# Retention's first projection tiles inside the prompt's attention, and the sample rows scaled before the constants arrive

## The reference

```python
h = rms_norm(x, g_mix[l])
proj = jnp.einsum('bld,de->ble', h, w_in[l])
rq, rk, rv, rg, mq, mk, mv, gate_r, gate_a = split_proj(proj)
rq = retnet_rotate(rq.reshape(B, L, R_HEADS, R_DK), pos)
rk = retnet_rotate(rk.reshape(B, L, R_HEADS, R_DK), pos) * (R_DK ** -0.5)
ro, r_state = ret_mix(l, rq, rk, rv)              # chunkwise retention
mq = rope(mq.reshape(B, L, M_HEADS, M_DH), pos)
mk = rope(mk.reshape(B, L, M_HEADS, M_DH), pos)
mo = attn_mix(l, mq, mk, mv)                      # block-sparse softmax attention
merged = sigmoid(gate_r) * (ro @ w_br_ret[l]) + sigmoid(gate_a) * (mo @ w_br_att[l])
x = x + merged @ w_out[l]
x = x + (silu(gate) * up) @ w_down[l]             # gate, up = rms_norm(x, g_ffn[l]) @ w_gu[l]
```

## Time and profile before

| | us |
|---|---|
| median of three runs | 2099.04 |
| profiled execution, its own time | 2107.27 |
| its span, first to last instruction | 2105.7 |
| TensorE busy in the span (matmuls) | 2042.1 |
| VectorE busy | 972.5 |
| ScalarE busy | 685.5 |
| GpSimd busy | 127.5 |

### The profile page before, as it was taken

One profiled execution on the slowest core, in us unless ns is written; L12 is line 12 of the kernel. 1 busy time (PEld: TensorE's weight loads), 2 busy tenths in 40 slices (PEclk: granted clock), 3 DMA queues, 4 the chain that ended last, 5 costly groups with the idle time before them and its releaser, 6 DMA issues.

```text
span 2105.7 us, 45102 instructions
## 1 busy us (share of the span) xinstructions
PE 2042.1 (97%) x17393; PEld 1913.4 (91%) x17393; DVE 972.5 (46%) x1620; ACT 685.5 (33%) x1054; POOL 127.5 (6%) x211
## 2 busy tenths in 40 slices
PE   6989999999999999999999899999999999999999
PEld 5958878988999999999988688789899999999998
DVE  5573522456445544543354643133654544444433
ACT  4365423223223222222233654222322322222222
POOL 0001120011000000000000011200100000000000
PEclk9999999999999999999999999999999999999999
DMA  6316683245333233223344266813543323232222
GB/s 191 121 43 212 191 276 106 81 141 171 102 109 93 80 91 89 80 70 95 95 132 139 68 209 205 292 42 99 159 145 110 91 81 99 80 89 78 83 82 90
DMA packets 257967, 253.20 MB, mean 120 GB/s; under 512 B 12266, under 2 KB 223378, under 8 KB 257554
## 3 DMA queue, kind: packets, MB, share of 16 engines
q1 hardware_dynamic: 240050, 190.68, 29.7%
q0 software_dynamic: 17632, 60.31, 9.0%
q10 hardware_dynamic: 128, 0.15, 0.0%
HBM read 230.52 MB, written 20.58 MB: 119 GB/s over the span
## 4 chain that ended last, share of the span: by engine, by line
PE 90%; DVE 3%; issue 2%; ACT 2%; DMA 2%; SPq 1%; ACTq 0%; DVEq 0%; POOL 0%; POOLq 0%
PE PS L626 61%; PE PS L607 3%; PE PS L765 3%; PE PS L608 2%; PE PS L609 2%; PE PS L588 2%; PE PS L589 2%; PE PS L590 2%; PE PS L776 1%; PE PS L825 1%; PE PS L567 1%; PE PS L722 1%; DMA CL<-in_consts_layer 1%; PE PS L736 1%; PE PS L659 1%
## 5 line engine op out<-in xcount | busy, mean ns | idle before, releaser
L626 PE MATMUL PS<-XH,WH 128*128 128x272 f32 x2176 | 455.2, 290 | 5.0 <-DVE EA L1698 3.1
L626 PE MATMUL PS<-XH,WL 128*128 128x272 f32 x2176 | 451.1, 289 | 0.0
L626 PE MATMUL PS<-XL,WH 128*128 128x272 f32 x2176 | 449.4, 288 | 0.0
L1405 DVE TENSOR_TENSOR WL<-RAW,WH 128x2048 fp32r<-128x2048 f32 (+2 forms) x144 | 310.7, 2158 | 244.0 <-ACT WH L1045 243.2
L626 PEld LDWEIGHTS PS<-XH,WH 128*128 128x128 f32 x2176 | 342.2, 189 | 12.6 <-DVE EA L1698 8.2
L626 PEld LDWEIGHTS PS<-XL,WH 128*128 128x128 f32 x2176 | 342.1, 189 | 0.0
L626 PEld LDWEIGHTS PS<-XH,WL 128*128 128x128 f32 x2176 | 339.9, 189 | 0.0
L1045 ACT ACTIVATE WH<-RAW 128x2048 fp32r<-128x2048 f32 (+2 forms) x152 | 274.6, 1806 | 91.0 <-PE PS L626 88.0
L1647 DVE TENSOR_TENSOR EA<-PS,RSTDB 128x544 f32<-128x544 f32 x120 | 86.4, 722 | 227.0 <-PE PS L626 226.3
L1242 ACT ACTIVATE EB<-EA 128x544 f32<-128x544 f32 x92 | 60.5, 658 | 329.7 <-DVE EA L1647 276.0
L607 PE MATMUL PS<-WH,XH 128*128 128x256 f32 x512 | 152.3, 298 | 0.0
(11 more groups left out here) (266 smaller groups left out, 3071.6 us busy)
## 6 DMA issues: line engine op xcount, KB each, us to landing
RAW<-in_w_in SPq DMA_DIRECT2D x106, 512.0 KB, 4.5
RAW<-in_w_gu SPq DMA_DIRECT2D x88, 512.0 KB, 4.8
PG<-in_cache_k SPq DMA_DIRECT2D x64, 256.0 KB, 3.3
PG<-in_cache_k POOLq DMA_DIRECT2D x64, 256.0 KB, 3.3
RAW<-in_w_down SPq DMA_DIRECT2D x32, 384.0 KB, 3.3
PG<-in_cache_v SPq DMA_DIRECT2D x44, 256.0 KB, 4.7
PG<-in_cache_v POOLq DMA_DIRECT2D x44, 256.0 KB, 5.0
RAW<-in_w_down SPq DMA_DIRECT2D x32, 320.0 KB, 3.7
```

The costliest lines, as they stand in the source:

```text
L626: last = pe.matmul(PS[:, 2 * pair + h, 0:HALF], w[:, i, c0:c0 + P], x[:, k, h * HALF:(h + 1) * HALF], start=first and i == 0 and a == 0, s ...
L1405: dve.tensor_tensor(WL[:, slot, 0:n], RAW[:, slot, 0:n], WH[:, slot, 0:n].bitcast(F32), ALU.subtract).then_inc(lo_ready, 1)
```

## The change

1. **The head of a layer.** The copy of the sample rows to `XTD` is issued by ScalarE at the top of the layer, no more by SyncE. SyncE loads `CL` right behind the first two units, and saves the prompt's rows behind the third unit's load. VectorE scales `XN` before it waits for `CL`.
2. **The prompt's attention.** `spread` comes behind `scores(0)` and `scores(1)`, `take_rt` behind `row_max(0)` and `row_max(1)`. Then follows `rqk` tile 0, now a full tile, in PSUM bank 1; ScalarE reads it out in step 2, VectorE rotates it behind the attention. `rqk` tile 1, the sample tile of the first unit, runs in step 15 between `attend(14)` and `turn_probs(15)`.
3. **The two later stages.** All other `rqk` tiles run one place earlier. The last one no longer stands at the start of the value stage. The first value step holds `rv` tiles 0, 1 and 2, and each later tile moves up by one step, so that the last step holds none. Splits and four weight loads move with them.

```diff
-ORDER0 = tuple(range(TT - 2)) + (TT - 1, TT - 2)
+ORDERS = {"mqk": tuple(range(TT - 2)) + (TT - 1, TT - 2), "rqk": (0, TT - 1) + tuple(range(1, TT - 1))}
...
+    def row_bank(name, f):
+
+        return 1 if (name, f) == ("rqk", 0) else (6, 3)[f % 2]
...
-        u, i = divmod(g * N_PAGES + p, TT - 1)
-        return [u * TT, u * TT + 1] if i == 0 else [u * TT + 1 + i]
+        step, out = g * N_PAGES + p, []
+        for r in ((0, 1) if step == 0 else (step + 1,) if step + 1 < 4 * (TT - 1) else ()):
+            u, i = divmod(r, TT - 1)
+            out += [u * TT, u * TT + 1] if i == 0 else [u * TT + 1 + i]
+        return out
...
-        return q + 1 if q < N_PAGES else q + 3
+        return q + 2 if q < N_PAGES else q + 4
...
-            hold(sp, x_lo, lay * NX + KT)
-            sp.dma_start(XTD.ap()[:, :, SEQ:N], XN).then_inc(xs_kept, 16)
             hold(sp, tile_done, lay * NT + 1)
             sp.dma_start(CL[:], consts_layer).then_inc(cl_in, 16)
-            sp.dma_start(XTD.ap()[:, :, 0:SEQ], XT[:, :, 0:SEQ]).then_inc(xt_kept, 16)
             for j in range(2):
                 full(U0["mqk"] + 2 + j, j, w_in, KT, C_MQ + (2 + j) * UC)
+                if j == 0:
+                    hold(sp, x_lo, lay * NX + KT)
+                    sp.dma_start(XTD.ap()[:, :, 0:SEQ], XT[:, :, 0:SEQ]).then_inc(xt_kept, 16)
...
-                for at_r, name, j, col in ((2, "rqk", 2, C_RQ), (8, "rqk", 3, C_RQ), (12, "rv", 0, C_RV),
-                                           (16, "rv", 1, C_RV), (20, "rv", 2, C_RV), (24, "rv", 3, C_RV),
-                                           (28, "br_att", 0, C_GA)):
+                for at_r, name, j, col in ((2, "rqk", 2, C_RQ), (7, "rqk", 3, C_RQ), (12, "rv", 0, C_RV),
+                                           (15, "rv", 1, C_RV), (20, "rv", 2, C_RV), (23, "rv", 3, C_RV),
+                                           (27, "br_att", 0, C_GA)):
...
             transposes([rows_of(QK, j) for j in range(8)], 0, sample_kv)
-            spread(2 * lay + 1, (6, 7))
...
             scores(0)
             scores(1)
+            spread(2 * lay + 1, (6, 7))
+            pe.wait_ge(own_act, lay * 2 + 2)
+            token_part("rqk", 0, kk)
             for s in range(16):
                 if s + 2 < 16:
                     scores(s + 2)
                 if s:
                     attend(s - 1)
+                if s == 15:
+                    pe.wait_ge(s_exp, lay * 16 + 15)
+                    token_part("rqk", 1, kk)
                 turn_probs(s)
...
             turn_sample_probs(0)
-            token_part("rqk", 19, kk)
...
+            act.wait_ge(x_lo, lay * NX + KT)
+            act.dma_start(XTD.ap()[:, :, SEQ:N], XN).then_inc(xs_kept, 16)
             for u in range(4):
...
+                if s == 2:
+                    to_rotate(0)
...
+                if f == 2 * TT - 1:
+                    split_at("rqk", 3)
...
             sample_probs_turned(0)
-            to_rotate(19)
             exp_group(1)
...
                 ahead("mqk", u // 2, u % 2)
                 if u == 0:
+                    dve.wait_ge(xs_kept, lay * 16 + 16)
+                    dve.tensor_tensor(XN, XN, GT[:, bass.ds(lay * KT, KT)].unsqueeze(2).to_broadcast([P, KT, NS]),
+                                      ALU.mult).then_inc(xn_ready, 1)
                     dve.wait_ge(cl_in, lay * 16 + 16)
...
             row_max(0)
             row_max(1)
+            take_rt(2 * lay + 1, (6, 7))
```

More of the change, by code:

```diff
@@ L29, with row_tile @@
 ORDER = (TT - 1,) + tuple(range(TT - 1))
-ORDER0 = tuple(range(TT - 2)) + (TT - 1, TT - 2)
+ORDERS = {"mqk": tuple(range(TT - 2)) + (TT - 1, TT - 2), "rqk": (0, TT - 1) + tuple(range(1, TT - 1))}
 KG = P // NS
-def row_tile(f, first=False):
-    return f // TT, (ORDER0 if first and f < TT else ORDER)[f % TT]
+def row_tile(name, f):
+    return f // TT, (ORDERS.get(name, ORDER) if f < TT else ORDER)[f % TT]
 UC = 256
@@ L370, in unit @@
                 if isinstance(u, int) and 2 <= u < U0["br_att"] + 2:
-                    hold(sp, tile_done, lay * NT + T0["mqk"] + (u - 2) * TT + (ORDER0.index(TT - 1) if u == 2 else 0) + 1)
+                    hold(sp, tile_done, lay * NT + T0["mqk"] + (u - 2) * TT + {2: ORDERS["mqk"].index(TT - 1), U0["rqk"] + 2: ORDERS["rqk"].index(TT - 1)}.get(u, 0) + 1)
                 for dst, src in parts:
@@ L571, in first_tile @@
             def first_tile(f):
-                u, t = row_tile(f, True)
+                u, t = row_tile("mqk", f)
                 n = ROWS[t]
@@ L593, in token_part @@
             def token_part(name, f, ks):
-                u, t = row_tile(f)
+                u, t = row_tile(name, f)
                 n = ROWS[t]
@@ L598, in token_part @@
                 wl = WL[:, u % 2, :].rearrange("p (k c) -> p k c", c=UC)
-                out = PS[0:n, (3, 6)[f % 2], 0:UC]
+                out = PS[0:n, row_bank(name, f), 0:UC]
                 if ks[0] == 0:
@@ L603, in token_part @@
                 if t == TT - 1:
-                    last = sample_part(u, (3, 6)[f % 2], (0, 1) if len(ks) == KT else (ks[0] // 4,))
+                    last = sample_part(u, row_bank(name, f), (0, 1) if len(ks) == KT else (ks[0] // 4,))
                 for k in ks if t < TT - 1 else ():
@@ L731, in attend @@
                     pe.wait_ge(mo_lo, lay * 4 + hp - 1)
+                elif t == 0 and hp == 0:
+                    pe.wait_ge(own_act, lay * 2 + 1)
                 elif t == 0:
-                    pe.wait_ge(own_act, lay * 2 + hp + 1)
+                    pe.wait_ge(tile_free, lay * NT + T0["rqk"] + 3)
                 for kt in range(t + 1):
@@ L786, in key_scores @@
                     last.then_inc(sc_done, 1)
-            token_part("rqk", 0, kk)
             pe.wait_ge(mo_lo, lay * 4 + 4)
@@ L793, in _ @@
                 if q == N_PAGES:
-                    token_part("rqk", N_PAGES + 1, kk)
                     token_part("rqk", N_PAGES + 2, kk)
+                    token_part("rqk", N_PAGES + 3, kk)
                 if q + 1 < NG * N_PAGES:
@@ L1061, in to_rotate @@
             def to_rotate(f):
-                u, t = row_tile(f)
+                u, t = row_tile("rqk", f)
                 act.wait_ge(tile_done, lay * NT + T0["rqk"] + f + 1)
                 act.wait_ge(rot_free, lay * 40 + 20 + f + 1)
-                act.activation(XS[:, f % 2, :], PS[:, (3, 6)[f % 2], 0:UC], ACT.Copy,
+                act.activation(XS[:, f % 2, :], PS[:, row_bank("rqk", f), 0:UC], ACT.Copy,
                                scale=(RT if u < 2 else RTK)[:, t:t + 1]).then_inc(tile_free, 1)
@@ L1079, in _ @@
                 for f in range(u * TT, (u + 1) * TT):
-                    t = row_tile(f, True)[1]
+                    t = row_tile("mqk", f)[1]
                     done(T0["mqk"] + f)
@@ L1088, in _ @@
                 for f in range(j * TT, (j + 1) * TT):
-                    t = row_tile(f)[1]
+                    t = row_tile("mv", f)[1]
                     value_tile("mv", f, MV[:, t, :] if t < TT - 1 else MVP, first_bank(4 * TT + f))
@@ L1170, in _ @@
             split_at("rqk", 1)
-            to_rotate(0)
+            to_rotate(1)
             keys_turned(0, range(GRP))
@@ L1174, in _ @@
                 if q == N_PAGES:
-                    to_rotate(N_PAGES + 1)
-                    split_at("rqk", 3)
                     to_rotate(N_PAGES + 2)
+                    to_rotate(N_PAGES + 3)
                 if q + 1 < NG * N_PAGES:
@@ L1481, in _ @@
                 last.then_inc(tr_dve, 1)
-            take_rt(2 * lay + 1, (6, 7))
             def row_max(s):
@@ L1582, in sample_probs_turned @@
                 dve.tensor_copy(PTS[g][0:NS, 8, :], PS[0:NS, 2, 0:P]).then_inc(pts_dve, 1)
+            rotated(0)
             split_at("rqk", 1)
-            rotated(0)
+            rotated(1)
             for q in range(NG * N_PAGES):
@@ L1588, in _ @@
                     select(0)
-                    rotated(N_PAGES + 1)
-                    split_at("rqk", 3)
                     rotated(N_PAGES + 2)
+                    rotated(N_PAGES + 3)
                     inverse_sum(0)
@@ L1600, in _ @@
             sample_probs_turned(0)
-            rotated(19)
             inverse_sum(1)
```

12 lines of the change are left out of this document (4 added, 8 removed).

## The result

| | median us | spread, runs | profiled execution |
|---|---|---|---|
| before | 2099.29 | 2096.23 to 2104.84, 20 | 2107.27, span 2105.7 |
| after | 2104.34 | 2101.02 to 2107.79, 20 | 2102.82, span 2101.2 |

The changed kernel takes 1.0023 of the time before (95% interval 1.0015 to 1.003): 3.1 to 6.3 us slower, where 2.2 us faster (2096.8 against 2099.04) was forecast. The time lies above the forecast's range. Note the last column: in the two profiled executions the changed kernel is the faster one by 4.5 us. The profiled execution of before was slower than every one of its 20 timed runs, that of after is among its faster ones. Much of what follows comes from that.

The account below looks back on a forecast made before the run. TensorE, busy 97% of the span, was taken as the bound, so only its stops and lower clock could change. Terms -8.0 - 4.9 + 2.1 + 8.4 = -2.4 us gave 2096.8 us against 2099.04, range 2090.5 to 2102.5.

Parts of the forecast that it names:

- The head (-8.0): Head of both layers: stops of 2.18 and 2.83 us and 1.5 us of lower clock each go, 8.0 us gained.
- The carry-over: Whole kernel: the -2.4 us worked out on the profiled 2107.27 us applies unchanged to the median of 2099.04.
- The attention (-4.9 + 2.1): Prompt's attention, both layers: 4.9 us gained at its start by filling idle time, 2.1 lost at its end.
- The shift at the start: Start of the prompt's attention: a full tile of 3.05 us delays the chain by only 0.6, gaining 2.45 per layer.
- The tail's 1.05: End of the prompt's attention: the sample tile, moved ahead of `turn_probs(15)`, loses 1.05 us per layer.
- The key stage (0): Key stage: the moved split of unit 3 costs nothing; up to 1 us a layer if its cover fails.
- The value stage (+8.4): Start of the value stage: a new 2.7 us TensorE stop plus 1.5 of lower clock per layer, 8.4 us lost.
- attention takes nothing for free: Rival: attention carries every inserted piece in full, losing 6.8 us at its end; +4.7, 2103.7 us, slower; chance 14%.

Follow-up runs that it names:

- e1: Kernel before with only the head's part of the change (sample rows copied by ScalarE and scaled before the constants, early `CL` load): 2097.74 us, ratio 0.9982.
- e0: Kernel before, unchanged, profiled once more: 2101.19 us, ratio 1.0006; profiled execution 2100.78 us.
- e2: Changed kernel with the head's part undone, leaving the attention's tiles and the shifted later stages: 2107.03 us, ratio 1.0024.
- e5: Kernel before with only `spread` and `take_rt` moved behind scores 0 and 1 and their `row_max`, no tile moved: 2097.58 us, ratio 0.999.
- e4: Changed kernel with the first `rv` read-out ahead of `exp_group(1)` and the `CL` load held until x's low halves are written: 2094.72 us, ratio 0.9966.
- e6: Changed kernel with the first `rv` read-out ahead of `exp_group(1)` and the sample tile back behind `attend(15)`: 2094.45 us, ratio 0.9972.
- e7: Kernel before with the head's part, late `CL` load, and `spread` and `take_rt` behind scores 0 and 1; no `rqk` tile moved: 2094.87 us, ratio 0.9969.
- e8: Changed kernel with first `rv` read-out ahead of `exp_group(1)`, late `CL` load and sample tile back behind `attend(15)`: 2092.37 us, ratio 0.996.
- e9: Changed kernel, unaltered, timed again on the chip of another group of runs: 2103.81 us, ratio 1.0015.
- e3: Changed kernel with ScalarE reading out the first `rv` tile ahead of `exp_group(1)` instead of behind it: 2096.01 us, ratio 0.9976.

## Why the prediction was wrong

**What the profiles add up to.** Means over the layers of all profiled executions that share the piece in question (in brackets how many layers; for the changed head those with the early load):

| stretch, per layer | old form | changed form | old - changed | forecast |
|---|---|---|---|---|
| head, layer 0 (first matmul to second sample tile) | 17.8 (5) | 16.1 (5) | 1.7 | 3.7 |
| head, layer 1 | 17.8 (5) | 16.3 (5) | 1.5 | 4.3 |
| attention to first keys, and the full tile that left the value stage | 56.9 + 3.05 (8) | 58.2 (10) | 1.7 | 1.4 |
| value stage, `turn_sample_probs(0)` to the last product with `MVS`, the full tile that left it added | 76.5 (8) | 76.8 + 3.05 (6) | -3.4 | -4.2 |

**The head (-8.0) is the step that failed.** e1 measured -3.8 by its ratio and -2.5 by its medians, and the table's two rows give -3.2. In layer 0 the step read a stop of 2.18 us and 1.5 us of lower clock from one execution. The stop depends on when `CL` lands; in five executions with the old head it was 2.0 to 2.2 us in three, where `CL` landed 8.4 to 8.5 us after its issue, 0.47 in e0 and absent in e2, where it landed after 6.8 and 7.0. The gain is real in three of five only. In layer 1 the old stop was 2.4 to 2.8 us in four of them and 0.99 in one (e5, `CL` landed after 7.0 us). There the step said: "`CL` ... is issued as soon as the last tile of layer 0 is done", and counted that as nothing. That early issue held up ScalarE by about 2.5 us (5.3 us idle on average against 2.75 with the late load), its rounding of the weight unit and with it the scaling, so that 2.05 us of stop remained in place of 2.83. e4 shows it: with the load held back, that head is 2.4 us shorter.

**The carry-over failed with it.** "A difference in single waits carries over unchanged" from 2107.27 to 2099.04 can hold only if the waits removed are also in an execution of 2099. They were not all there: e0's profiled execution, 2100.78 us against a median of 2100.27, has only 0.47 us of layer 0's stop and lacks the clock losses behind it and behind one of the third scores. The 8.2 us between profile and median should have been split among the very terms of the sum. Set against its own execution the sum gives 2107.27 - 2.4 = 2104.9, near the 2104.34 measured. That is luck and no support for the sum: the two profiled executions differ by 4.5 us, not 2.4, and in medians the sign is the other.

**The attention (-4.9 + 2.1).** The shift at the start was worked out as 0.6, since the old third scores took 1.31 us at the lower clock. Against e0's layer 1, where they took 0.92, it is 1.3. The tail's 1.05 is exact (e6: 1.0). So the gain is 0.75 a layer against that layer, and 1.7 on average over the executions, as seven of the eight third scores in the old order have the lower clock behind their stop and none of the ten in the new. In the profile that the forecast used, both layers also had a second piece at the lower clock near the end of the attention (from 156.4 and 1190.7 us), which no term priced. So the stretch to the first keys, forecast to grow by 1.6 us, took 58.17 us in that profile and 58.07 in the one of after. -1.5 to -3.5 for -2.8: the size was acceptable; the cause, that the tile fills the hole, was wrong, for `spread` does (e5).

**The key stage (0).** Pages of keys came late by 0.10 to 0.81 us in several executions of the new load order, by 0.52 once before, and by 2.03 in e7 with the old load order. The stage took 95.6 us on average before (e7 left out) and 96.1 after, 95.9 with e4 and e8 counted in: 0.6 to 0.9 us in all. Whether the new load order is the cause isn't settled, since e7's kernel has late pages too.

**The value stage (+8.4)** was right in place, releaser and size: 2.53 us for 2.7, and half clock behind it at 3 of 6 stops (both of e2, one of e9, none of the first profile). The table's average over the traces is 6.7 us, and e3 puts it between 6.1 and 9.9. The Trainium skill (TensorE: Matmul & The Clock Gate, section on HAM oscillation) lets each group behind a wait start cold; the waits of its example are for DMA and take some 3 to 5 us, longer than this stop. Here that is borne out by three of the six.

**Sum.** The terms give 2099.04 - 2.4 = 2096.6; the forecast's 2096.8 is a slip of 0.2. With the head at -3.8 (e1's ratio) its sum is +1.8, with -2.5 (e1's medians) +3.1. The two halves measured apart give +1.2 by ratios (-3.8 + 5.0) and +4.2 by medians (-2.5 + 6.8). The change measured +4.8 [3.1, 6.3] in the first comparison and +3.2 [0.8, 5.5] in e9's. So the timed runs can't tell whether anything beyond the named terms is left. The traces can't settle it either: the rows of the table and the key stage add up to about +1, so 2 to 4 us of the measured loss are in no trace here. The profiled executions of after (2102.82 and 2100.69) lie below its medians, and no trace shows a typical one. The lower clock behind both value stops, as in e2, would be 3 us of it, but that is argued, not shown. The rival "attention takes nothing for free" had the nearest time, 2103.7, for a reason that the traces don't bear out.

## What to carry to other kernels

Before a sum of waits is set against a median, compare the profiled execution with the spread of the timed runs. If it lies outside, the waits it shows are in part that execution's own, and each term must say in how many executions it exists. Before a tile goes into a hole, look for a short piece of the same chain that fills it; here 1.4 us of `spread` took the hole, and a 3 us tile then paid nearly full price. A transfer issued early is not free: ask what else must come in over the DMA engines at that moment. And a read-out that frees a bank goes ahead of an exponential that is wanted later.

## What the runs showed of the hardware

- A load of 1188.5 KB under way at the turn of a loop lengthens ScalarE's unexplained idle time there from 1.84 to 2.12 us to 4.87 to 5.62 us (2.57 to 2.85 with the load held back and the save issued by ScalarE).
- In all five executions with that load under way no instruction packet started between its first packet and 0.2 us before its last.
- The same TensorE stop of 2.53 us was followed by half clock three times in six occurrences (three executions, two layers each). Of the stops of 2.03 to 2.83 us at the heads 8 of 9 were, of the 1.72 us stops before the third scores 7 of 8, of the 1.50 us stop in the key stage none, and of the 1.6 to 2.1 us stops ahead of layer 1's first matmul none. All but one of these stretches lasted 3.4 us at half speed, which costs 1.7 us of TensorE's work; one (e0, layer 1's head) lasted 6.8. The length of a stop alone does not decide it; what does stays open.
- The load of `CL` landed 6.8 to 8.8 us after its issue in the executions of the old head; the stop of 2.2 us in layer 0 came or went with it.
- The kernel of e8 varies less than the one before, as far as its 6 runs tell: 2090.5 to 2094.8 us against 2095.2 to 2106.0 in 17.
